# Two transformer blocks with gathered experts: choices packed into units 1 to 4, a denser second product, a gate product written token innermost

## The reference

```python
def peer(h, w_query, sub_keys_1, sub_keys_2, expert_down, expert_up):
    q = (ht @ w_query).reshape(t_, PEER_HEADS, 2, PEER_HALF)     # 8 heads, halves of 128
    s1 = einsum('thd,hkd->thk', q[:, :, 0], sub_keys_1)          # 128 keys each
    s2 = einsum('thd,hkd->thk', q[:, :, 1], sub_keys_2)
    v1, i1 = top_k(s1, 16);  v2, i2 = top_k(s2, 16)
    cand = v1[..., :, None] + v2[..., None, :]                   # 256 pairs
    top_s, pos = top_k(cand, 16)
    idx = take(i1 * 128 + i2, pos)                               # of 16384 experts
    gate = softmax(top_s)
    act = einsum('tkd,td->tk', expert_down[idx], h)
    w = gate * gelu(act)
    return einsum('tk,tkd->td', w, expert_up[idx])               # added to x
```

## Time and profile before

| | us |
|---|---|
| median of three runs | 4122.43 |
| lowest and highest | 4111.66, 4123.57 |
| profiled execution, device time | 4114.45 |
| its span on the core | 4112.7 |

### The profile page before, as it was taken

The page is one execution under the profiler, slowest core; times in us unless marked ns, Lnnn a source line. Parts: engine busy times, 40 slices in busy tenths (PEclk is TensorE's granted clock), DMA queues, the critical chain, the costliest instruction groups (busy, mean ns, idle before and its releaser), DMA issues. The chain is left out here.

```text
span 4112.7 us, 41028 instructions
## 1 busy us (share of the span) xinstructions
PE 3346.1 (81%) x13955; PEld 1703.8 (41%) x13955; DVE 2393.2 (58%) x4239; ACT 830.1 (20%) x1960; POOL 1646.3 (40%) x1133
## 2 busy tenths in 40 slices
PE   7998988999868887556877889888688875568887
PEld 6343434444755554112222257457555541122222
DVE  3787875410297777776555422411877778765553
ACT  1222224300110002772000012221100117730000
POOL 0000000000046656788666500000366667886764
PEclk9999999999989988667999989979899987679899
DMA  6343432343369999899999953413699989999998
GB/s 218 108 127 100 129 116 90 103 136 133 133 226 375 377 361 362 322 353 361 374 380 379 367 197 101 143 61 123 225 362 372 372 337 319 341 336 373 379 368 333
DMA packets 317005, 1066.64 MB, mean 259 GB/s; under 512 B 95634, under 2 KB 104674, under 8 KB 215906
## 3 DMA queue, kind: packets, MB, share of 16 engines
q0 software_dynamic: 147456, 717.84, 46.1%
q1 hardware_dynamic: 134240, 335.05, 23.1%
q10 hardware_dynamic: 35120, 11.33, 1.2%
HBM read 1417.99 MB, written 2.10 MB: 345 GB/s over the span
## 5 line engine op out<-in xcount | busy, mean ns | idle before, releaser
L2007 DVE CUSTOM_DVE_ANT_0 sc<-big,hs 128x2048 f32<-128x2048 f32 x512 | 1174.6, 2294 | 658.5 <-DMA big<-in_peer_down,sc 328.8
L699 PE MATMUL bank<-wring,ht 128*128 128x512 f32 (+1 forms) x1792 | 791.4, 600 | 2.4 <-ACT ht L1235 1.7
L1067 PE MATMUL bank<-big,sc 128*32 128x512 f32 x4096 | 647.7, 716 | 106.8 <-DVE sc L2026 57.2
L1006 PE MATMUL bank<-wring 128*128 128x512 f32 x1024 | 536.9, 660 | 98.2 <-DMA wring<-in_dense_up 82.5
L633 POOL DMA_INDIRECT big<-in_peer_up,sc x256 | 419.5, 1639 | 272.3 <-PE bank L1067 138.4
L989 PE MATMUL bank<-ht,wring 128*128 128x256 f32 x2048 | 518.9, 406 | 0.0
L699 PEld LDWEIGHTS bank<-wring,ht 128*128 128x128 f32 x1792 | 342.0, 194 | 421.0 <-issue 415.2
L633 POOL DMA_INDIRECT big<-in_peer_u,sc x256 | 414.9, 1621 | 214.6 <-DVE sc L1981 92.3
L633 POOL DMA_INDIRECT big<-in_peer_v,sc x256 | 395.5, 1545 | 262.7 <-PE bank L1067 123.1
L989 PEld LDWEIGHTS bank<-ht,wring 128*128 128x128 f32 x2048 | 398.2, 201 | 209.8 <-issue 156.5
L633 POOL DMA_INDIRECT big<-in_peer_down,sc x256 | 391.1, 1528 | 234.0 <-DVE sc L1981 93.1
(11 more groups left out here) (376 smaller groups left out, 2852.1 us busy)
## 6 DMA issues: line engine op xcount, KB each, us to landing
wring<-in_w_in SPq DMA_DIRECT2D x84, 1024.0 KB, 5.7
wring<-in_dense_down SPq DMA_DIRECT2D x64, 1024.0 KB
wring<-in_dense_up SPq DMA_DIRECT2D x256, 256.0 KB
wring<-in_w_out SPq DMA_DIRECT2D x32, 1024.0 KB, 5.0
wring<-in_w_attn_o SPq DMA_DIRECT2D x16, 1024.0 KB, 5.0
wring<-in_peer_w_query SPq DMA_DIRECT2D x16, 1024.0 KB, 4.8
wring<-in_peer_w_q SPq DMA_DIRECT2D x16, 1024.0 KB, 4.8
wring<-in_glu_w_a SPq DMA_DIRECT2D x8, 1024.0 KB, 5.0
```

The source lines that it names most:

```text
L699: mm = pe.matmul(dense_bank[2 * pair + t][:, 0:w_cols], lhs[:, k, t * P:(t + 1) * P], wslot[:, b, kk * w_cols:(kk + 1) * w_cols], start=(k ...
L1006: mm = pe.matmul(dense_out[t][:, :], dense_w[:, r, t * P:(t + 1) * P], sup[:, m % 2, r % 4, :], start=(r == 0), stop=(r == DENSE - 1))
L1067: mm = pe.matmul(acc_bank[j][32 * q:32 * q + 32, :], w_blocks[:, u % 2, g, :], gslot[:, m % RING, q * 512:(q + 1) * 512], start=(u % PH == ...
L2007: v.tensor_tensor_reduce(dot_out, gslot[:, m % RING, :], h[:, u // PH, :], 1.0, 0.0, ALU.mult, ALU.add, sub(rAC)[:, i:i + 1]).then_inc(dot ...
```

## The change

1. The choices of units 2 to 15. Before, unit u held the choices of units 2u + 2 and 2u + 3, from u = 0 on, each over eight steps: keys in steps 0 and 2, pairs in 4, decode in 6. Now `ahead_at` gives four steps to each choice from n = 16 on: both keys in the first, pairs in the second, decode in the third, turning of the indices on PE in the fourth. So units 1 to 3 hold four choices each, the first half of unit 4 two, and unit 0 none. Before, the last choice was in steps 104 to 110; now it is in 68 to 70. PE's `turn_indices` of units 2 and 3 ahead of its loop go, as does ScalarE's `peer_soft` of unit 2 behind score chunk 12.
2. The second token tile: its selections are turned at n = 134 (was 118), its 16 gate batches are at 136 to 166 (were 133 to 163). The wait for them moves from PE to VectorE.
3. `up_part` runs at 3 parts for 2 steps (was 4 for 3) from n = 169 to 254 (was 165 to 260).
4. `take_gates` writes the same product in the order p, r, n: the 16 tokens innermost, instead of the 32 keys.

```diff
+def ahead_at(n):
+    u, part = divmod(n - TOPK, 4)
+    return (u + 2, part) if n >= TOPK and u + 2 < UNITS else (None, part)
+
 def turned_at(n):
-    u, g = divmod(n, GRP)
-    return 2 * u + 2 + g // 8 if u and g % 8 == 7 and 2 * u + 2 + g // 8 < UNITS else None
+    u, part = ahead_at(n)
+    return u if part == 3 else None
...
-GATE_AT = {101 + 2 * i: i for i in range(GATE_N)} | {133 + 2 * i: GATE_N + i for i in range(GATE_N)}
-FIRST_UP = 165
+GATE_AT = {101 + 2 * i: i for i in range(GATE_N)} | {136 + 2 * i: GATE_N + i for i in range(GATE_N)}
+FIRST_UP = 169
...
-    return min(max(n - FIRST_UP, 0) * 4 // 3, 4 * DENSE)
+    return min(max(n - FIRST_UP, 0) * 3 // 2, 4 * DENSE)
...
             def turn_selections(layer, t):
                 if t:
-                    pe.wait_ge(gate_evac, layer * GRP + 4)
+                    pe.wait_ge(gate_evac, layer * GRP + GRP // 2)
...
             def expert_products(layer):
-                turn_indices(base + 2)
                 pe.wait_ge(stage_t_ready, base + 2)
                 for i in range(quarter_at(0)):
                     down_quarter(layer, i)
-                turn_indices(base + 3)
...
-                    if i in (9, 10, 12):
-                        u = {9: 0, 10: 1, 12: 2}[i]
-                        peer_soft(layer * UNITS + u, u % 2)
+                    if i in (9, 10):
+                        peer_soft(layer * UNITS + i - 9, i - 9)
...
             def first_one_hots(layer, hb):
+                if hb % GATE_N == 0:
+                    v.wait_ge(sel_ready, 2 * (layer * NT + t + 1))
...
             def take_gates(layer, b):
-                w = dense_w[:, :, b * 16:(b + 1) * 16].rearrange("p r n -> p n r")
-                v.tensor_tensor(w, gate_bank[:, 0:16 * DENSE].rearrange("p (n r) -> p n r", r=DENSE), w,
+                w = dense_w[:, :, b * 16:(b + 1) * 16]
+                v.tensor_tensor(w, gate_bank[:, 0:16 * DENSE].rearrange("p (n r) -> p r n", r=DENSE), w,
                                 ALU.mult).then_inc(gate_evac, 1)
...
             def peer_units(layer):
-                        ahead, part = 2 * u + 2 + k // 8, k % 8
-                        if part == 4 and ahead - 1 < UNITS:
-                            collect(base + ahead - 1, ahead - 1)
-                        if ahead < UNITS:
-                            if part in (0, 2):
-                                choose_keys(layer, ahead, part // 2)
-                            elif part == 4:
+                        if n == 4:
+                            collect(base + 1, 1)
+                        if turned_at(n - 2) is not None:
+                            collect(base + turned_at(n - 2), turned_at(n - 2))
+                        ahead, part = ahead_at(n)
+                        if ahead is not None:
+                            if part == 0:
+                                choose_keys(layer, ahead, 0)
+                                choose_keys(layer, ahead, 1)
+                            elif part == 1:
                                 choose_pairs(ahead)
-                            elif part == 6:
+                            elif part == 2:
                                 decode(base + ahead, ahead)
-                        if n in (85, 119):
-                            take_selections(layer, int(n == 119))
+                        if n in (85, 135):
+                            take_selections(layer, int(n == 135))
```

More of the change, by code:

```diff
@@ L1051, in turn_gates @@
                     pe.wait_ge(gate_evac, n)
-                if b == 4:
-                    pe.wait_ge(sel_ready, 2 * (layer * NT + 2))
                 for j in range(4):
@@ L1090, in expert_products @@
                             turn_indices(base + turned_at(n))
-                        if n in (84, 118):
-                            turn_selections(layer, int(n == 118))
+                        if n in (84, 134):
+                            turn_selections(layer, int(n == 134))
                         if u:
@@ L1470, in peer_units @@
                     for k in range(TOPK):
-                        n, ahead = u * TOPK + k, 2 * u + 2 + k // 8
-                        if k % 8 == 4 and 3 <= ahead < UNITS:
+                        n = u * TOPK + k
+                        ahead, part = ahead_at(n)
+                        if ahead is not None and part == 1:
                             peer_soft(base + ahead, ahead % 2)
```

## The result

| | us |
|---|---|
| changed kernel, median of 9 runs | 4147.94 (4130.27 to 4171.3) |
| kernel before, median of 9 runs beside it | 4117.77 (4109.34 to 4123.57) |
| ratio | 1.0081, 95% interval [1.0062, 1.01] |
| profiled execution of the changed kernel, device time and span | 4149.8, 4148.1 |

A forecast was written before the change was run, and what follows sets the result against it. Transfers were taken to bound most stretches, VectorE dots 0 to 15, with TensorE late in the tail. Layer terms of -5 and -11 us, together -16, took the median 4122.43 to 4106 us, range 4078 to 4138.

The forecast's parts named there:

- 1, first unit free: Dots 0 to 15: bare dots without choices take 38.1 us, -24.4 us in each layer.
- POOL is shut out: First unit: gather issues meet dots, 3.1 us each, 16 are 12 us longer per layer; 4130, chance 0.04.
- 2, four choices to a unit: Dots 16 to 71: VectorE becomes the limit at 5.4 us a step; 310 us, +33 and +40.
- The first rival: Dots 16 to 71: packed choices starve the ring and dots wait; 4148 at 1.5 us per block, chance 0.16.
- 3, after dot 72: Dots 72 to 95: landed ring lets VectorE run ahead, 106 us, -11 each; dots 96 to 111: -9 and -7.
- no lead after dot 72: Dots 72 to 95 keep the rate of before, so the two -11 are gone; 4128, chance 0.18.
- 4, gates and product: Dots 112 to 165: later gate batches cost 1 us a layer (0 to 4); product 0.9 to 1.2 us, off the path.
- 5, the dense rate: Dots 166 to 254: three parts for two steps, transfers still the limit; +3.5 us in each layer.
- The tail: After dot 255: second layer 34 us instead of 47.2, -13; first layer +2 (bounds -11 to +5).
- My terms of 22, 2.6 and 8 us: Second layer after dot 255: 13 outstanding rows, output's first half, last row to end; given as 34 us.
- The sum: Whole kernel: -5 us in the first layer, -11 in the second, together -16; 4106 by the median.

The follow-up runs named there:

- the finer ring: Changed kernel with the second dense product's staging cut into four buffers of two parts instead of two of four: 4112.91 us, ratio 0.9996.
- the same ring: Kernel before, still at four parts for three steps, with that staging in four buffers of two parts instead of two of four: 4115.7 us, ratio 1.0003.

## Why the prediction was wrong, step by step

**1, first unit free: right.** 38.0 us against 38.1. No issue of POOL held it: the free unit's dots stand 2.33 us apart. The rival "POOL is shut out" didn't come: the issues took 2.03 us each beside the dots, not 3.1. In the trace of before, 414 of the 1,024 issues took 1.4 us or more; every one of them had begun during a dot and ended some 0.87 us after that dot's end.

**2, four choices to a unit: right.** 312.8 and 313.5 us against 310. The first rival would have been visible as waits for rows between the pieces of a choice. VectorE was busy 293.6 of 313 us in layer 1, and in that stretch the trace has no wait of it for gathered rows (48.7 us before). The median of 4147.94 is nearly that rival's 4148, but by accident: the cause is another, in another stretch.

**3, after dot 72: the lead was mis-sized.** -2.0 and -6.6 us instead of -11 twice. Three dots found their rows landed; then VectorE waited. Its timeline from dot 72 on:

```profile
1499.72 2.29 DVE L2008 CUSTOM_DVE_ANT_0 sc<-big,hs 128x2048 f32<-128x2048 f32 x1
1502.05 2.29 DVE L2008 CUSTOM_DVE_ANT_0 sc<-big,hs 128x2048 f32<-128x2048 f32 x1
...
1504.85 2.29 DVE L2008 CUSTOM_DVE_ANT_0 sc<-big,hs 128x2048 f32<-128x2048 f32 x1 [0.40 <-DMA big<-in_peer_down,sc]
1513.85 2.29 DVE L2008 CUSTOM_DVE_ANT_0 sc<-big,hs 128x2048 f32<-128x2048 f32 x1 [6.71 <-DMA big<-in_peer_down,sc]
```

Behind the three dots the rows come at the transfers' pace: 115 us at 380 GB/s are 43.7 MB, all 24 steps of 1.82 MB, where I had put 21.5 steps at 390 GB/s and 5 us of latency. No row showed that rate or that latency; here the next row was waited for 6.7 us. And there was no lead in bytes. By the start of dot 72 of layer 1, 94.6 MB of gathered rows had come, and 94.4 MB before the change; in the stretch itself 34.4 MB came in both. A landed ring is worth the few dots whose rows it holds, and it is paid back if the ring is as full at the end of the stretch as at its start. My rival "no lead after dot 72" had this right, at least in layer 1. Dots 96 to 111 gave -11.6 and -7.4 (predicted -9 and -7; 16 steps at 4.1 us are 66, not the 67 of the working).

**4, gates and product: right where it matters.** Dots 112 to 165 changed by -1.4 and +3.9 us (predicted +1, bounds 0 to 4), so the first lies outside the bounds; kernels that leave this stretch alone lie between 221.6 and 225.3 us in layer 1 and between 218.4 and 224.3 in layer 2. The product took 686 ns instead of my 0.9 to 1.2 us, hidden as foreseen.

**5, the dense rate: this step failed.** I had +3.5 in each layer and measured +16.9 and +18.4. The working asked whether the transfers carry the bytes and whether TensorE's work fits into a step of 4.7 us; both were true, as the finer ring shows. It did not ask how long a buffer of four parts takes to come back, though the trace of before had 82.5 us of waits for just these rows. The row was on the page, and no group of mine has it:

```profile
L1006 PE MATMUL bank<-wring 128*128 128x512 f32 x1024 | 536.9, 660 | 98.2 <-DMA wring<-in_dense_up 82.5 <-issue 9.3 <-DVE xs L2047 6.3
```

and after the change:

```profile
L1011 PE MATMUL bank<-wring 128*128 128x512 f32 x1024 | 539.5, 664 | 130.5 <-DMA wring<-in_dense_up 125.1
```

In layer 1 the waits grew by 30.4 us (38.9 to 69.3) for 16.9 us of time, in the second by 12.2 us (43.7 to 55.9) for 18.4. So no price per microsecond of wait holds: at four for three all of it could be taken away for nothing. Why is in part argued. By the times of single instructions TensorE's work in a step was 1.33 x 1.85 + 1.0 = 3.5 us of 4.7, and at three for two it is 3.8. Measured over dots 169 to 232 of layer 1, it was busy 3.85 us of a step of 4.77 before, with 0.48 us of waits for dense rows; after, 4.04 us of 4.92, with 0.75. What is left of a step beside these two falls from 0.44 to 0.13 us, so nearly nothing was left to catch up with before a gather was late. In the second layer it was small already and falls from 0.16 to 0.12 us, so that averages don't carry the account there. Shown by runs is that the rate makes the loss, that the finer ring takes it away, and that the same ring gains nothing at the old rate.

**The tail.** In the second layer -4.8 us instead of -13. TensorE did become free early, as forecast; but more was left to move: 42 us at 299 GB/s are 12.6 MB, 10.5 of gathered rows (15 of 0.7 MB) and 2.1 of the output, where I had taken 13 rows and 8.6 MB of them (before it was 8.7). My terms of 22, 2.6 and 8 us also add up to 32.6, not to the 34 that I wrote. With the finer ring 9.9 MB of rows were left and the tail was 40.3 us, so most of the mis-sizing has nothing to do with the buffers' wait. The 1.9 MB more are some 5 us at the 390 GB/s of my 22 us; the rest is that transfers went slower than I took them, since the DMA share was 0.77 in this tail. What held them there was not tested. In layer 1 it was +4.3 instead of +2, inside its bounds. The bytes were as foreseen (16.8 MB for 17), at 349 GB/s where I had taken 400, a rate that no row shows; and 43 us against 44, which I had written, is not +2.

**The sum.** From predicted -5 to measured +16.8 in layer 1: 13.4 of it are the rate, 9 the lead, 2.3 the tail, 2.2 the choices, against -5.0 from the gates and dots 96 to 111. From -11 to +22.2 in the second: 14.9 the rate, 8.2 the tail, 4.4 the lead, 3.3 the choices, 2.9 the gates. Half of the miss is one step. What stays open: in both layers' dots 72 to 95 the traces show that the lead isn't kept, but no run changed the ring's depth; and I didn't try five steps to a unit, which would show how close to the transfers' pace a choice may come.

## What to carry to other kernels

Before a rate is raised, read the waits of the engine that gets the work, also where they cost nothing now, and ask how much of its step is left over once they grow; a buffer that comes free only after its last piece can be the cheaper thing to mend, as it was here. When work is moved out of one stretch, price the steps where it lands as a rate (work and dot per step) against the rate of what limits them there: four steps to a choice were 5.4 us against 4.8 and cost all that was won, six were 4.4 and cost nothing. A full ring is a lead only for the steps whose rows it holds: eight slots at two rows a step gave three dots here.

## What the runs showed of the hardware that I had not expected

A VectorE product of 128x512 that reads PSUM at a stride of 128 bytes (token innermost, one number from each of 16 rows of 32) and SBUF in runs of 16 numbers took 686 ns, as a contiguous one did (684 ns). The same product with the bank contiguous and SBUF at a stride of 1 KB, in and out, took 1,214 ns. The stride on the PSUM side cost nothing, that on the SBUF side 0.53 us. The prediction had carried the rule of the Trainium skill (SBUF — State Buffer, "Door 1: The DMA port swizzle") on lines of 8 bytes in PSUM over from matmuls to VectorE; for this read the measurement shows no such cost.
